# Router logits in plain fp32 from the residual, and 14 cells of the first expert's weights fetched earlier

## The chip, the cores and the metric

The kernel runs on one core of a Trainium2 chip. The metric is the device time of one execution, in microseconds; the median of several executions counts.

## What is computed

A trunk of two decoder layers over 256 tokens of width 1024, in fp32. Layer 0 is differential attention and a dense SwiGLU, layer 1 is an attention over blocks (here one block of 256, so plain causal attention with ALiBi) and a top-2-of-8 expert SwiGLU. The part that the change touches is the second layer's feed-forward:

```python
def moe_swiglu(h, router, w_gate, w_up, w_down):
    ...
    logits = (tok @ router).astype(jnp.float32)
    top_v, top_i = lax.top_k(logits, TOP_K_EXPERTS)
    w = jax.nn.softmax(top_v, axis=-1)
    gates = jnp.sum(jax.nn.one_hot(top_i, N_EXPERTS, dtype=jnp.float32) * w[..., None], axis=1)
    out = jnp.zeros_like(tok)
    for e in range(N_EXPERTS):
        out = out + gates[:, e:e + 1].astype(tok.dtype) * swiglu(tok, w_gate[e], w_up[e], w_down[e])
```

`tok` is the normalized residual. Each expert has w_gate and w_up of 1024x3584 and w_down of 3584x1024, 44 MB together, and all eight are read: 352 MB.

## The kernel before

**Weights and the ring.** All weights stream from HBM through a ring in SBUF of 7 slots of 8 cells; a cell is 128x512 fp32 (256 KB). SyncE issues the transfers in program order. Before each it waits until `group_used`, which TensorE counts up as it uses cells, says that the cells to be overwritten are done with. `NG` is the count at the end of the last product before the experts (attention's output projection of layer 1).

**Items.** The experts' work is cut into items. Item 0, 2, 4, 6 and 7 are "few" items (up to 64 tokens, plain fp32 products straight from the ring, `few_columns` and `few_down`), items 1, 3 and 5 are "big" ones (up to 128 tokens; ScalarE copies each cell to a rounded high half `whi`, VectorE subtracts it to a low half `wlo`, and TensorE makes three products, lines 1725 to 1727). The tokens of each expert decide which expert is worked on in which item; GpSimd builds the table. An item has 24 steps: gate's eight row blocks of seven cells, up's eight of seven cells, down's seven of eight cells: 168 cells in all (56 + 56 + 56). The big item's and the following few item's steps are interleaved in SyncE's and TensorE's order.

**Item 0.** Its expert is fixed (expert 0), so that its weights can be fetched before routing is known (`few_item(0, 0, ...)`, lines 701 to 728). Cells 0 to 55, all of gate, go to the ring. Cells 56 to 71, up's first two row blocks and two cells of the third, go to two further buffers, `ahead[0]` and `ahead[1]` of eight cells each, which share memory with tiles that are not in use at the time: `ahead[0]` with `whi`, `ahead[1]` with part of attention's tiles (q and k halves, values) and with `hhi`, `hlo`, `ihi` and `ilo`. Cells from 72 on go to the ring again, where gate's were. `few_used` gives the count for which SyncE waits, one for each row block; the block that holds cells of `ahead[1]` waits for `logit_mm` too.

**The router.** While the output projection of layer 1 ends, VectorE adds it to the transposed residual `resT` (`add_block`, lines 1598 to 1609). ScalarE rounds `resT` to high halves, put in `hhi` and `ihi` (`raw_hi`, line 981), VectorE subtracts for low halves, in `hlo` and `ilo` (`raw_lo`, line 1592). The router's weights `rt` are halved too, side by side in `rt_parts` (16 columns). TensorE (`logits`, line 1985) multiplies with `rt_parts` as the loaded operand, two products for each of eight row blocks, which gives 16 rows of 256 tokens. ScalarE copies them out (`logitT`, line 1002), and two small products with `sum_parts` (line 1997) turn them and add the halves: 128 tokens x 8 experts in `psA`, twice. VectorE finds the top two (lines 1615 to 1622) and sets `member`; TensorE counts the tokens of each expert (lines 2004 to 2008), VectorE makes `pick` from it (line 1626), and TensorE gathers item 0's rows with it (`gather_first`, line 2015). Between these, TensorE turns the residual back to rows (`turn_rows`, line 1974, 16 transposes), which ScalarE copies and squares (lines 1004 and 988) and VectorE copies (line 1631), and `keep_streaming` (line 1979) is a filler product. The first product of item 0 is at line 2100.

Of the kernel before, what the change touches and what calls it, by code (L numbers as in the profile page):

```python
# [30 lines left out]
P = 128  # L31
# [10 lines left out]
def trunk(nc, x, norm_mix, norm_ffn, diff_w_qkv, diff_w_o, diff_lambda, diff_subln, moba_w_qkv, moba_w_o,  # L42
# [143 lines left out]
    with ExitStack() as ctx:  # L186
        def sb(name, shape, dt=F32, stack=ctx):
            return stack.enter_context(nc.sbuf_tensor(name, shape, dt))

        def sem(name):  # L190
            return ctx.enter_context(nc.semaphore(name))
# [82 lines left out]
        sum_parts = sb("sum_parts", [2 * E, E])  # L274
        rs_of_slot = sb("rs_of_slot", [P, 1])
        ident_r = sb("ident_r", [P, P], F32R)
        rt_parts = sb("rt_parts", [P, KD, 2 * E], F32R)
        top = sb("top", [P, TB, E])
        top_at = sb("top_at", [P, TB, E], U32)
        logitT = sb("logitT", [2 * E, T])  # L280
# [103 lines left out]
        rt_split = sem("rt_split")  # L384
        block_done = sem("block_done")
        block_added = sem("block_added")
        thi_done = sem("thi_done")
        tlo_done = sem("tlo_done")
# [4 lines left out]
        logitT_out = sem("logitT_out")  # L393
# [56 lines left out]
        def blocks(t, first, n):  # L450
            return t[:, first:first + n, :].rearrange("p k t -> p (k t)")

        def T_part(which, first, n):
            return blocks(hid_parts(first // 4)[which], first % 4, n)

        def f(ap):
            return ap.bitcast(F32)
# [49 lines left out]
        def few_runs(i, j):  # L507
            runs = []
            for q in range(item_cells[j]):
                x = item_from[j] + q  # L510
                if isinstance(i, int) and i == 0 and CELLS <= x < CELLS + AHEAD_CELLS:
                    what, at = divmod(x - CELLS, GS)
                    what = 1 + what
                else:
                    what, at = 0, ring_cell(i, x)
                if runs and runs[-1][0] == what and runs[-1][1] + runs[-1][2] == at:
                    runs[-1][2] += 1
                else:
                    runs.append([what, at, 1, q])
            return [([ring_all, ahead[0], ahead[1]][what][:, at * W:(at + n) * W], q, n) for what, at, n, q in runs]  # L520

        def few_used(j):
            end = item_from[j] + item_cells[j]
            if end <= CELLS:
                return NG - CELLS + -(-end // GS) * GS
            return NG + max(end - CELLS - AHEAD_CELLS if end < 2 * CELLS + AHEAD_CELLS else end - CELLS, 0)
# [122 lines left out]
        def _(sp):  # L649
# [52 lines left out]

            def few_item(i, e, slots_of):
                for j in slots_of:
                    kind, at = item_slots[j]
                    first = isinstance(i, int) and i == 0
                    if first:
                        sp.wait_ge(group_used, few_used(j))
                        if item_from[j] <= CELLS + GS < item_from[j] + item_cells[j]:
                            sp.wait_ge(logit_mm, 1)  # L710
                    else:
                        sp.reg_add(used_past, used_past, item_cells[j])
                        sp.wait_ge(group_used, used_past)
                    if kind != "down":
                        w = moe_w_gate if kind == "gate" else moe_w_up
                        for to, q, n in few_runs(i, j):
                            sp.dma_start(to, w[0][e, at * P:(at + 1) * P, q * W:(q + n) * W]).then_inc(item_full[j], 16)
                        continue
                    dst = few_runs(i, j)[0][0]
                    if not isinstance(i, int) and j >= FS - 2:  # L720
                        for a, (b, half, g) in enumerate(DOWN_ROWS[at]):
                            sp.dma_start(dst[:, a * D:(a + 1) * D], few_down(e, b, half)[:, g * D:(g + 1) * D]).then_inc(
                                piece_full[j - FS + 2][a] if a < FBW - 1 else item_full[j], 16)
                        continue
                    for a, (b, half, g) in enumerate(DOWN_ROWS[at]):
                        if g == 0:
                            rows = BANKS[b] // P
                            sp.dma_start(dst[:, a * D:(a + rows) * D], few_down(e, b, half)).then_inc(item_full[j], 16)
# [21 lines left out]
        def _(act):  # L750
# [183 lines left out]
            act.wait_ge(rt_gained, 1)  # L934
            nc.scalar.copy(rt_parts[:, :, 0:E], rt[:, :, :]).then_inc(rt_split, 1)
# [44 lines left out]
            def raw_hi(first, n):  # L980
                nc.scalar.copy(T_part(0, first, n), blocks(resT, first, n)).then_inc(thi_done, n)

# [9 lines left out]
            for q in range(2):  # L992
                act.wait_ge(block_added, 2 * q + 2)
                raw_hi(2 * q, 2)
            act.wait_ge(block_added, 6)
            raw_hi(4, 2)
            for k in range(6, KD):
                act.wait_ge(block_added, k + 1)
                raw_hi(k, 1)
            row_square(0, 0)  # L1000
            act.wait_ge(logit_mm, 1)
            nc.scalar.copy(logitT[:, :], psA[0:2 * E, 0, 0:T]).then_inc(logitT_out, 1)
# [96 lines left out]
        def _(pool):  # L1099
# [73 lines left out]
            tt(sum_parts[:, :], ident[0:2 * E, 0:E], ident[0:2 * E, E:2 * E], ALU.add).then_inc(scales_set, 1)  # L1173
# [3 lines left out]
            pool.wait_ge(scales_set, 3)  # L1177
# [138 lines left out]
        def _(dve):  # L1316
# [273 lines left out]
            def raw_lo(first, n):  # L1590
                dve.wait_ge(thi_done, first + n)
                nc.vector.tensor_tensor(T_part(1, first, n), blocks(resT, first, n), f(T_part(0, first, n)),
                                        ALU.subtract).then_inc(tlo_done, n)

            halve_to(NG)
            dve.wait_ge(rt_split, 1)
            nc.vector.tensor_tensor(rt_parts[:, :, E:2 * E], rt[:, :, :], f(rt_parts[:, :, 0:E]),
                                    ALU.subtract).then_inc(rt_split, 1)
# [5 lines left out]
            for q in range(2):  # L1604
                raw_lo(2 * q, 2)
# [4 lines left out]
            raw_lo(4, 2)  # L1610
            for a in range(2):
                raw_lo(6 + a, 1)
            dve.wait_ge(logit_mm, 2)
# [106 lines left out]
        def _(pe):  # L1720
# [260 lines left out]
            def logits(first, last):  # L1981
                for k in range(first, last):
                    pe.wait_ge(tlo_done, k + 1)
                    for which in (0, 1):
                        ins = mm(psA[0:2 * E, 0, 0:T], rt_parts[:, k, :], T_part(which, k, 1),
                                 start=k == 0 and which == 0, stop=k == KD - 1 and which == 1)
                return ins

            pe.wait_ge(rt_split, 2)
# [4 lines left out]
            pe.wait_ge(scales_set, 3)  # L1994
            pe.wait_ge(logitT_out, 1)
            for tb in range(TB):
                ins = mm(psA[:, 1, tb * E:(tb + 1) * E], logitT[:, tb * P:(tb + 1) * P], sum_parts[:, :], start=True, stop=True)
            ins.then_inc(logit_mm, 1)
# [255 lines left out]
```

## Time and profile before

| | us |
|---|---|
| median of 3 executions | 1258.49 (1257.98 to 1259.1) |
| profiled execution | 1259.62 |
| its span, first to last instruction | 1257.8 |
| TensorE busy | 1234.0 (98%) |
| VectorE, ScalarE, GpSimd busy | 641.3, 562.0, 99.8 |
| read from HBM | 422.23 MB |
| TensorE's granted clock | 0.999 of full |

Times in a profile count from the first instruction of the span. The 1.8 us that the execution is longer than its span lie around it. A queue's name ends in q (SPq is SyncE's): such a row is the time in which transfers were issued, not the one in which they moved.

### The profile page before, as it was taken

The page shows a single profiled execution, that of the slowest core. Times are in us where ns is not written, and L with a number is a line of the kernel's source. Part 1 is how long each engine was busy: PE and PEld are TensorE (multiplying, and loading weights), DVE is VectorE, ACT ScalarE, POOL GpSimd, SP SyncE. Part 2 cuts the span into 40 slices and gives each one's busy share as a digit, 9 for nine tenths or more (in the row PEclk, how much of TensorE's full clock was granted, in tenths as well). Part 3 has the DMA queues.
Part 4 walks back from the last instruction along what each step waited for, and adds up shares of the span by engine and source line. Part 5 has one row for each costly group of instructions (what it writes and reads, how often), then busy time and mean ns, then how long its engine had stood idle before and what let it go on. Part 6 is the DMA issues. An engine that isn't in the chain of part 4 may idle for free.

```text
span 1257.8 us, 18674 instructions
## 1 busy us (share of the span) xinstructions
PE 1234.0 (98%) x7266; PEld 872.8 (69%) x7266; DVE 641.3 (51%) x788; ACT 562.0 (45%) x895; POOL 99.8 (8%) x260
## 2 busy tenths in 40 slices
PE   9998999999999999999999999999999999999887
PEld 8988999999999954487575457848447765733232
DVE  5787765555765400288383257838126855620011
ACT  6565454443655421388173158527027835500001
POOL 1000000000000074100001200000210000021000
PEclk9999999999999999999999999999999999999999
DMA  9933545357632299999999999999999999999997
GB/s 329 378 136 135 182 167 188 134 166 234 228 118 100 96 426 428 422 424 427 426 426 427 424 425 426 425 426 425 428 422 426 427 407 418 424 429 424 427 427 291
DMA packets 72136, 424.48 MB, mean 337 GB/s; under 512 B 5457, under 2 KB 24050, under 8 KB 48242
## 3 DMA queue, kind: packets, MB, share of 16 engines
q1 hardware_dynamic: 71696, 422.76, 83.0%
q8 instruction: 58, 0.95, 0.3%
q10 hardware_dynamic: 354, 0.54, 0.1%
q14 instruction: 28, 0.23, 0.0%
HBM read 422.23 MB, written 1.05 MB: 337 GB/s over the span
## 4 chain that ended last, share of the span: by engine, by line
PE 89%; DMA 5%; ACT 2%; DVE 2%; issue 1%; POOLq 0%; POOL 0%; ACTq 0%; DVEq 0%; SPq 0%
PE psB L2100 10%; PE psY L2115 9%; PE psA L2100 7%; PE psY L1725 7%; PE psY L1727 7%; PE psY L1726 7%; PE psB L1725 6%; PE psA L1725 5%; PE psB L1727 5%; PE psB L1726 5%; PE psA L1727 5%; PE psA L1726 5%; DMA ring<-in_moe_w_up 2%; DMA ring<-in_moe_w_down 2%; PE psY L2066 1%; PE psY L1873 1%
## 5 line engine op out<-in xcount | busy, mean ns | idle before, releaser
L1585 DVE TENSOR_TENSOR wlo<-ring,whi 128x2048 fp32r<-128x2048 f32 (+3 forms) x171 | 289.1, 1727 | 150.7 <-ACT whi L950 148.5
L950 ACT CAST whi<-ring 128x1024 fp32r<-128x1024 f32 (+1 forms) x276 | 259.5, 981 | 155.1 <-DMA ring<-in_moe_w_down 72.4
L1332 DVE TENSOR_TENSOR wlo<-ring,whi 128x1024 fp32r<-128x1024 f32 (+2 forms) x104 | 152.3, 1485 | 17.6 <-ACT whi L764 17.5
L764 ACT CAST whi<-ring 128x1024 fp32r<-128x1024 f32 (+1 forms) x134 | 133.4, 1023 | 60.0 <-PE psY L1727 28.3
L2100 PE MATMUL psB<-ring,resT 128*64 128x512 f32 x620 | 149.0, 598 | 7.4 <-DMA ring<-in_moe_w_up 5.4
L2100 PE MATMUL psA<-ring,resT 128*64 128x512 f32 (+1 forms) x624 | 113.9, 486 | 0.0
L1725 PE MATMUL psA<-xhi,whi 128*128 128x256 f32 x368 | 105.0, 285 | 2.6 <-DVE wlo L1332 1.2
L2100 PEld LDWEIGHTS psA<-ring,resT 128*64 128x64 f32 x624 | 44.8, 137 | 89.1 <-issue 89.1
L1725 PE MATMUL psB<-xhi,whi 128*128 128x256 f32 x368 | 106.4, 289 | 0.0
L1726 PE MATMUL psA<-xlo,whi 128*128 128x256 f32 x368 | 102.7, 279 | 0.0
L1726 PE MATMUL psB<-xlo,whi 128*128 128x256 f32 x368 | 102.7, 279 | 0.0
L1727 PE MATMUL psA<-xhi,wlo 128*128 128x256 f32 x368 | 102.6, 279 | 0.0
L1727 PE MATMUL psB<-xhi,wlo 128*128 128x256 f32 x368 | 102.6, 279 | 0.0
L2100 PEld LDWEIGHTS psB<-ring,resT 128*64 128x64 f32 x620 | 41.6, 136 | 75.7 <-issue 56.8
L1652 DVE TENSOR_TENSOR rowbuf<-psY,rowbuf 128x512 f32<-128x512 f32 x28 | 18.6, 688 | 141.1 <-PE psY L2066 141.1
L2115 PE MATMUL psY<-ring,hidT 128*64 128x512 f32 x320 | 72.1, 596 | 0.7 <-DMA ring<-in_moe_w_down 0.6
L1725 PEld LDWEIGHTS psA<-xhi,whi 128*128 128x128 f32 x368 | 69.2, 188 | 4.5 <-issue 3.3
L1725 PEld LDWEIGHTS psB<-xhi,whi 128*128 128x128 f32 x368 | 69.4, 189 | 0.0
L1726 PEld LDWEIGHTS psB<-xlo,whi 128*128 128x128 f32 x368 | 69.3, 188 | 0.0
L1726 PEld LDWEIGHTS psA<-xlo,whi 128*128 128x128 f32 x368 | 69.2, 188 | 0.1
L1727 PEld LDWEIGHTS psB<-xhi,wlo 128*128 128x128 f32 x368 | 69.2, 188 | 0.0
L1727 PEld LDWEIGHTS psA<-xhi,wlo 128*128 128x128 f32 x368 | 69.2, 188 | 0.0
(382 smaller groups left out, 2147.1 us busy)
## 6 DMA issues: line engine op xcount, KB each, us to landing
ring<-in_moe_w_down SPq DMA_DIRECT2D x50, 2048.0 KB, 15.6
ring<-in_moe_w_up SPq DMA_DIRECT2D x53, 1792.0 KB, 18.1
ring<-in_moe_w_gate SPq DMA_DIRECT2D x50, 1792.0 KB, 14.9
ring<-in_moe_w_gate SPq DMA_DIRECT2D x13, 1024.0 KB, 15.5
ring<-in_ffn_w_gate SPq DMA_DIRECT2D x5, 2048.0 KB, 8.8
ring<-in_ffn_w_up SPq DMA_DIRECT2D x5, 2048.0 KB, 7.8
ring<-in_ffn_w_down SPq DMA_DIRECT2D x5, 2048.0 KB, 8.0
ring<-in_moe_w_gate SPq DMA_DIRECT2D x13, 768.0 KB, 14.0
```

The lines of the kernel that those rows point to most:

```text
L764: nc.scalar.copy(hi_of(m, size), part_of(ring, s, g, size)).then_inc(hi_done, size)
L950: nc.scalar.copy(hi_of(NG + m, size), item_part(ring, m, size)).then_inc(hi_done, size)
L1332: nc.vector.tensor_tensor(part_of(wlo, s, g, size), part_of(ring, s, g, size), f(hi_of(m, size)), ALU.subtract).then_inc(lo_done, size)
L1585: nc.vector.tensor_tensor(item_part(wlo, m, size), item_part(ring, m, size), f(hi_of(NG + m, size)), ALU.subtract).then_inc(lo_done, size)
L1652: nc.vector.tensor_tensor(r, slot_bank(half), r, ALU.add).then_inc(add_done, 1)
L1725: mm(ps, xh, wh, start=start, stop=False, skip_group_check=shared)
L1726: mm(ps, xh, wl, start=False, stop=False, skip_group_check=shared)
L1727: return mm(ps, xl, wh, start=False, stop=stop, skip_group_check=shared)
L1873: ins = mm(psY[:, 3, i * wide:(i + 1) * wide], probsT[:, u % 2, i * (tb + 1) + kb, :], val[:, kb, c:c + wide], start=kb == 0, stop=kb == tb)
L2066: mm(slot_bank(half), s_, y, start=True, stop=True).then_inc(scatter_mm, 1)
L2100: ins = mm(few_bank(b)[half * FEW:(half + 1) * FEW, to:to + end - x], few_in[:, k, :], raw[:, x - q * W:end - q * W], start=k == 0, stop=k ...
L2115: ins = mm(psY[half * FEW:(half + 1) * FEW, 0, :], few_act[b][:, g * P + left * FEW:g * P + (left + 1) * FEW], raw[:, a * D + half * W:a * ...
```

## The change

The logits are computed from `resT` and `rt` in plain fp32, with `resT` as the loaded operand: for each of the eight row blocks two products of eight columns, one for each half of the tokens. They come out with tokens in rows, so that nothing is turned or added afterwards. The halves, `rt_parts`, `sum_parts`, `logitT` and their steps are gone from ScalarE, VectorE, GpSimd and TensorE.

`ahead[1]` no longer holds halves of the residual, and the two further buffers change places: cells 56 to 63 go to `ahead[1]`, 64 to 71 to `ahead[0]`. Cells 42 to 47 (gate's seventh row block without its last cell) wait for `group_used` as gate's sixth does. Behind them, once the last product of attention's weights and values is counted (`pv_done`), SyncE fetches up's first row block and one cell of the second, to `ahead[1]`. The last cell of gate's seventh row block follows when `NG` is reached. The count is now worked out for each transfer instead of each row block, and nothing waits for `logit_mm`.

```diff
-                if runs and runs[-1][0] == what and runs[-1][1] + runs[-1][2] == at:
+                last_dense = isinstance(i, int) and i == 0 and x == CELLS - GS
+                if runs and runs[-1][0] == what and runs[-1][1] + runs[-1][2] == at and not last_dense:
...
-            return [([ring_all, ahead[0], ahead[1]][what][:, at * W:(at + n) * W], q, n) for what, at, n, q in runs]
-
-        def few_used(j):
-            end = item_from[j] + item_cells[j]
+            return [([ring_all, ahead[1], ahead[0]][what][:, at * W:(at + n) * W], q, n) for what, at, n, q in runs]
+
+        def first_used(j, q, n):
+            end = item_from[j] + q + n
             if end <= CELLS:
                 return NG - CELLS + -(-end // GS) * GS
             return NG + max(end - CELLS - AHEAD_CELLS if end < 2 * CELLS + AHEAD_CELLS else end - CELLS, 0)
...
+            def early_ahead(j, q):
+                return CELLS <= item_from[j] + q < CELLS + GS
+
+            def first_rows(j, a):
+                to, q, n = few_runs(0, j)[a]
+                k = item_slots[j][1]
+                sp.dma_start(to, moe_w_up[0][0, k * P:(k + 1) * P, q * W:(q + n) * W]).then_inc(item_full[j], 16)
...
-                    if first:
-                        sp.wait_ge(group_used, few_used(j))
-                        if item_from[j] <= CELLS + GS < item_from[j] + item_cells[j]:
-                            sp.wait_ge(logit_mm, 1)
-                    else:
+                    if first and kind == "down":
+                        sp.wait_ge(group_used, first_used(j, 0, GS))
+                    elif not first:
...
                         for to, q, n in few_runs(i, j):
+                            if first and early_ahead(j, q):
+                                continue
+                            if first and item_from[j] + q == CELLS - GS:
+                                sp.wait_ge(pv_done, 2 * UNITS)
+                                first_rows(item_slot["up", 0], 0)
+                                first_rows(item_slot["up", 1], 0)
+                            if first:
+                                sp.wait_ge(group_used, first_used(j, q, n))
...
-            act.wait_ge(rt_gained, 1)
-            nc.scalar.copy(rt_parts[:, :, 0:E], rt[:, :, :]).then_inc(rt_split, 1)
...
-            def raw_hi(first, n):
-                nc.scalar.copy(T_part(0, first, n), blocks(resT, first, n)).then_inc(thi_done, n)
...
-            for q in range(2):
-                act.wait_ge(block_added, 2 * q + 2)
-                raw_hi(2 * q, 2)
-            act.wait_ge(block_added, 6)
-            raw_hi(4, 2)
-            for k in range(6, KD):
-                act.wait_ge(block_added, k + 1)
-                raw_hi(k, 1)
             row_square(0, 0)
-            act.wait_ge(logit_mm, 1)
-            nc.scalar.copy(logitT[:, :], psA[0:2 * E, 0, 0:T]).then_inc(logitT_out, 1)
...
-            def raw_lo(first, n):
-                dve.wait_ge(thi_done, first + n)
-                nc.vector.tensor_tensor(T_part(1, first, n), blocks(resT, first, n), f(T_part(0, first, n)),
-                                        ALU.subtract).then_inc(tlo_done, n)
...
             def logits(first, last):
                 for k in range(first, last):
-                    pe.wait_ge(tlo_done, k + 1)
-                    for which in (0, 1):
-                        ins = mm(psA[0:2 * E, 0, 0:T], rt_parts[:, k, :], T_part(which, k, 1),
-                                 start=k == 0 and which == 0, stop=k == KD - 1 and which == 1)
+                    pe.wait_ge(block_added, max(k + 1, 4))
+                    for tb in range(TB):
+                        ins = mm(psA[:, 1, tb * E:(tb + 1) * E], resT[:, k, tb * P:(tb + 1) * P], rt[:, k, :],
+                                 start=k == tb == 0, stop=k == KD - 1, skip_group_check=True)
                 return ins
 
-            pe.wait_ge(rt_split, 2)
+            pe.wait_ge(rt_gained, 1)
             logits(0, 4)
             turn_rows(0, 0)
             logits(4, KD).then_inc(logit_mm, 1)
             turn_rows(0, 1)
-            pe.wait_ge(scales_set, 3)
-            pe.wait_ge(logitT_out, 1)
-            for tb in range(TB):
-                ins = mm(psA[:, 1, tb * E:(tb + 1) * E], logitT[:, tb * P:(tb + 1) * P], sum_parts[:, :], start=True, stop=True)
-            ins.then_inc(logit_mm, 1)
```

Two places show how the order moves. First SyncE's queue from gate's sixth row block to up's third, before (the last three of "x6" are gate's sixth, seventh and eighth row block):

```order
L717 DMA ring<-in_moe_w_gate 128x3584 [waits group_used]
L717 DMA ring<-in_moe_w_gate 128x512 [waits group_used]
L717 DMA ring<-in_moe_w_gate 128x3072
L717 DMA ring<-in_moe_w_gate 128x3584 [waits group_used] x6
L717 DMA ahead<-in_moe_w_up 128x3584 [waits group_used]
L717 DMA ahead<-in_moe_w_up 128x512 [waits logit_mm,group_used]
L717 DMA ahead<-in_moe_w_up 128x3072
L717 DMA ahead<-in_moe_w_up 128x1024 [waits group_used]
L717 DMA ring<-in_moe_w_up 128x2560
```

The same in the changed kernel (line numbers are its own; the last of "x4" is gate's sixth row block):

```order
L722 DMA ring<-in_moe_w_gate 128x3584 [waits group_used] x4
L722 DMA ring<-in_moe_w_gate 128x3072 [waits group_used]
L700 DMA ahead<-in_moe_w_up 128x3584 [waits pv_done]
L700 DMA ahead<-in_moe_w_up 128x512
L722 DMA ring<-in_moe_w_gate 128x512 [waits group_used]
L722 DMA ring<-in_moe_w_gate 128x3584 [waits group_used]
L722 DMA ahead<-in_moe_w_up 128x3072 [waits group_used]
L722 DMA ahead<-in_moe_w_up 128x1024 [waits group_used]
L722 DMA ring<-in_moe_w_up 128x2560 [waits group_used]
```

Gate's seventh row block is cut in 3072 and 512 columns; between the pieces stand up's first row block and the first cell of its second, which stood behind gate's eighth.

Then TensorE's queue around the second half of the logits, before (L1985 the split products, L1974 the transposes, L1997 the sum of the halves, L2004 the first count):

```order
L1974 MATMUL psY<-ident,resT 128x128 x4
L1985 MATMUL psA<-ihi,rt_parts 16x256
L1985 MATMUL psA<-ilo,rt_parts 16x256
...
L1974 MATMUL psY<-ident,resT 128x128 x4
L1997 MATMUL psA<-sum_parts,logitT 128x8 x2
L1974 MATMUL psY<-ident,resT 128x128 x4
L1974 MATMUL psB<-ident,resT 128x128 x4
L1979 MATMUL psY<-resT,ident 128x128
L2004 MATMUL psA<-member,pickT 128x8
```

And the whole of it in the changed kernel (L1961 the logits, L1950 the transposes, L1955 keep_streaming, L1975 the first count):

```order
L1961 MATMUL psA<-rt,resT 128x8 x8
L1950 MATMUL psY<-ident,resT 128x128 x4
L1961 MATMUL psA<-rt,resT 128x8 x8
L1950 MATMUL psY<-ident,resT 128x128 x8
L1950 MATMUL psB<-ident,resT 128x128 x4
L1955 MATMUL psY<-resT,ident 128x128
L1975 MATMUL psA<-member,pickT 128x8
```

Sixteen products of 256 columns and two of eight are replaced by sixteen of eight columns, at the same places; the transposes stay, and eight of them now follow each other.

## Rows read from the trace of the kernel before

**Rows 1.** The page: TensorE's busy time; the dense layer's transfers, KB each, us to landing
```profile
PE 1234.0 (98%) x7266; PEld 872.8 (69%) x7266; DVE 641.3 (51%) x788; ACT 562.0 (45%) x895; POOL 99.8 (8%) x260
...
ring<-in_ffn_w_gate SPq DMA_DIRECT2D x5, 2048.0 KB, 8.8
```
**Rows 2.** Windows: length, busy of PE, PEld, DVE, ACT, POOL, clock, DMA share, GB/s
```profile
429.00:437.00 8.00, 7.91 (x68) 7.69 (x67) 3.90 (x7) 2.44 (x7) 1.94 (x23) 1.00 0.01 3
...
447.00:1160.00 713.00, 712.13 (x3366) 425.25 (x3368) 350.10 (x278) 315.88 (x425) 79.48 (x172) 1.00 1.01 424
...
1160.00:1236.50 76.50, 68.25 (x334) 24.50 (x331) 4.98 (x8) 6.24 (x17) 0.73 (x1) 1.00 1.00 425
```
**Rows 3.** TensorE's waits (total us, times, longest), 447 to 1160, then after 1160
```profile
PE psB L1725 <- DVE wlo L1585: 0.9, 3, 0.3
...
PE psB L2100 <- DMA ring<-in_moe_w_up: 5.4, 5, 1.1
```
**Rows 4.** Timeline of SyncE: start, length, queue, line, transfer, how many
```profile
422.35 15.53 SPq L717 DMA_DIRECT2D ring<-in_moe_w_gate  x3
...
437.07 0.80 SPq L717 DMA_DIRECT2D ring<-in_moe_w_gate  x2
...
450.78 14.99 SPq L717 DMA_DIRECT2D ring<-in_moe_w_up  x7
```
**Rows 5.** Issue to landing: at 385; L717 up to 432; at 450.8
```profile
ring<-in_moe_w_gate SPq DMA_DIRECT2D x1, 1792.0 KB, 6.8
...
DMA to landing us min/median/max: 2.7/7.2/7.5
...
ring<-in_moe_w_up SPq DMA_DIRECT2D x1, 1280.0 KB, 11.9
```
**Rows 6.** Issue to landing of the transfers issued at 609, 1028 and 1034
```profile
ring<-in_moe_w_gate SPq DMA_DIRECT2D x1, 1792.0 KB, 12.7
...
ring<-in_moe_w_gate SPq DMA_DIRECT2D x1, 1792.0 KB, 9.6
...
ring<-in_moe_w_down SPq DMA_DIRECT2D x1, 2048.0 KB, 9.7
```
**Rows 7.** Windows: the stretch behind the issue at 1034
```profile
1035.00:1040.00 5.00, 5.00 (x28) 1.90 (x26) 0.00 (x0) 0.00 (x0) 0.00 (x0) 1.00 0.94 313
```
**Rows 8.** DMA queues, 1034 to 1035: packets, MB, share of 16 engines
```profile
q8 instruction: 1, 0.02, 6.4%
```
**Rows 9.** Timeline of TensorE: attention's last product with values
```profile
423.43 1.10 PE L1873 MATMUL psY<-val,probsT 128*128 128x64 f32 x8 [0.24 <-ACT probsT L815]
```
**Rows 10.** Timeline of TensorE: first split product, first count, first product of item 0
```profile
436.87 0.28 PE L1985 MATMUL psA<-hhi,rt_parts 128*16 128x256 f32 x1
...
441.99 0.24 PE L2004 MATMUL psA<-member,pickT 128*128 128x8 f32 x1
...
447.14 0.65 PE L2100 MATMUL psB<-ring,resT 128*64 128x512 f32 x2
```
**Rows 11.** The chain of waits, in order of time: start, us, what
```profile
441.29 0.44 PE psB L1974 x4
...
443.22 1.82 PE psA L2015 x16
```
**Rows 12.** Groups of instructions, 443 to 446.9: busy us, mean ns of one
```profile
L2015 PE MATMUL psA<-pick,rowbuf 128*128 128x64 f32 x16 | 2.0, 276 | 0.0
```
**Rows 13.** Timelines of ScalarE and VectorE behind the logits
```profile
440.06 1.01 ACT L1004 COPY rowbuf<-psY 128x1024 f32<-128x1024 f32 x1
...
440.74 0.25 DVE L1615 MAX8 top<-psA 128x8 f32<-128x8 f32 x2 [1.64 <-PE psA L1997]
...
441.67 0.17 DVE L1622 TENSOR_TENSOR member<-chosen 128x16 fp32r<-128x16 f32 x1
...
443.69 0.68 DVE L1631 COPY rowbuf<-psB 128x512 f32<-128x512 f32 x1
```
**Rows 14.** Timeline of GpSimd: the first step behind the tables, its idle time ahead
```profile
492.55 0.19 POOL L1288 COPY slot_now<-few_slot_at 128x1 f32<-128x1 f32 x1 [11.28 <-ACT row_and_weight L1041]
```

More of the change, by code:

```diff
@@ L273, in trunk @@
         pickT = sb("pickT", [P, T], F32R)
-        sum_parts = sb("sum_parts", [2 * E, E])
         rs_of_slot = sb("rs_of_slot", [P, 1])
         ident_r = sb("ident_r", [P, P], F32R)
-        rt_parts = sb("rt_parts", [P, KD, 2 * E], F32R)
         top = sb("top", [P, TB, E])
         top_at = sb("top_at", [P, TB, E], U32)
-        logitT = sb("logitT", [2 * E, T])
         count = pickT[:, :].rearrange("p (a t) -> p a t", a=2)
@@ L383, in trunk @@
         rt_gained = sem("rt_gained")
-        rt_split = sem("rt_split")
         block_done = sem("block_done")
         block_added = sem("block_added")
-        thi_done = sem("thi_done")
-        tlo_done = sem("tlo_done")
         rowT_mm = sem("rowT_mm")
@@ L392, in trunk @@
         logit_mm = sem("logit_mm")
-        logitT_out = sem("logitT_out")
         count_set = sem("count_set")
@@ L451, in blocks @@
             return t[:, first:first + n, :].rearrange("p k t -> p (k t)")
-        def T_part(which, first, n):
-            return blocks(hid_parts(first // 4)[which], first % 4, n)
         def f(ap):
@@ L1172, in _ @@
             tt = nc.gpsimd.tensor_tensor
-            tt(sum_parts[:, :], ident[0:2 * E, 0:E], ident[0:2 * E, E:2 * E], ALU.add).then_inc(scales_set, 1)
             pool.wait_ge(sq_done, 4 * 3 + TB)
@@ L1176, in _ @@
             pool.wait_ge(pos_set, 1)
-            pool.wait_ge(scales_set, 3)
+            pool.wait_ge(scales_set, 2)
             link(tt(key[:, :], pos[:, TB, :], tie[:, :], ALU.add))
@@ L1588, in item_halve @@
                 return done
-            def raw_lo(first, n):
-                dve.wait_ge(thi_done, first + n)
-                nc.vector.tensor_tensor(T_part(1, first, n), blocks(resT, first, n), f(T_part(0, first, n)),
-                                        ALU.subtract).then_inc(tlo_done, n)
             halve_to(NG)
-            dve.wait_ge(rt_split, 1)
-            nc.vector.tensor_tensor(rt_parts[:, :, E:2 * E], rt[:, :, :], f(rt_parts[:, :, 0:E]),
-                                    ALU.subtract).then_inc(rt_split, 1)
             dve.wait_ge(block_done, 1)
@@ L1603, in _ @@
             add_block(psB[:, 0, :], 2, block_added, 2)
-            for q in range(2):
-                raw_lo(2 * q, 2)
             dve.wait_ge(group_used, NG)
@@ L1609, in _ @@
                 nc.vector.tensor_tensor(r, psB[:, 1, a * T:(a + 1) * T], r, ALU.add).then_inc(block_added, 1)
[L1610 to L1613, printed above, removed]
+            dve.wait_ge(logit_mm, 1)
             for tb in range(TB):
```

## Prediction

> **What bounds the kernel now.** I began with the page. TensorE works 98% of the span [rows 1]; the windows then show the DMA engines full as well from 447 us on, at about 425 GB/s [rows 2]. Two resources look like the bound at once, and which of them it is must be settled before a transfer that comes earlier can be given a price. From 429 to 437 us the DMA engines stand still (3 GB/s) [rows 2]: that is the hole which the change fills. From 447 to 1160 TensorE works 712.13 of 713 us [rows 2], and its waits there name VectorE's splits, 0.9 us, and no transfer [rows 3]. From 1160 to 1236.5 it works only 68.25 of 76.5 us [rows 2], and there it waits for weights, 5.4 us in one row alone [rows 3]. So TensorE sets the pace up to 1160, and the stream of weights sets the end.
>
> What ties the two is the ring. SyncE may issue a transfer only when TensorE has used up the cells that it overwrites. How far the stream's backlog covers this is read from issue to landing. A transfer of seven cells (1792 KB) that meets idle DMA engines lands after 6.8 to 7.5 us, 7.2 in the middle (the 2.7 is a single cell) [rows 5]: 4.3 us of data (1.835 MB at 424 GB/s) and 2.9 fixed. While the engines are full it takes longer, and the excess is the queue ahead of it. This excess shrinks: 12.7 us at 609, 9.6 at 1028, and the eight cells (2048 KB) at 1034 take 9.7 [rows 6]. Eight cells on idle engines should take 7.2 + 0.6 = 7.8 (bounds 6.8 + 0.6 = 7.4, and 8.8, the dense layer's transfers of that size [rows 1]). So some 1.9 us of queue is left at 1034 (bounds 0.9 and 2.3). The window there agrees: DMA share 0.94, 313 GB/s [rows 7]; some engines already run dry. On this place the forecast hangs.
>
> **The early transfers.** The 14 cells are 14 x 0.262 = 3.67 MB, 8.7 us of DMA. Six (gate's seventh slot without its last cell) wait for the same count as gate's sixth slot and go out right behind it, at 422.7 [rows 4]. The other eight wait for attention's last product, which ends at 423.43 + 1.10 = 424.5 [rows 9]. Behind the sixth slot's landing (422.35 + 7.2 = 429.5 [rows 4, 5]) they fill the engines to 438.2, and the hole is closed. The stream would be 8.7 us ahead. But little may follow: at 437.07 [rows 4] SyncE can issue 1 + 7 + 6 + 2 = 16 cells, 9.9 us of data, which run from 439 to 449. The 17th lies in gate's first slot, used up 3 us after item 0 starts; its issue is at 450.78 now [rows 4]. Here the engines run dry for some 2 us. Its transfer of five cells then lands at 451.3 + 2.9 + 3.1 = 457.3, against 450.78 + 11.9 = 462.7 [rows 4, 5]: the lead is 5.4 us, already 3.3 less. SyncE's new wait for pv_done holds behind it only transfers that wait for 437.07 anyway, and its wait for the logits, removed, held two that stood behind a full queue: neither moves anything.
>
> **The logits on TensorE.** Its path runs from the first split product at 436.87 to the first count (L2004) at 441.99, 5.12 us [rows 10]. In it stood 16 split products, the two that sum the halves, 16 transposes, two records of keep_streaming, and the waits for VectorE's splits, ScalarE's copy and member. In it will stand: the 16 transposes, 0.11 each by the row of four in 0.44, 1.76 us [rows 11]; keep_streaming's two, 0.22; and 16 fp32 products of eight columns with 128x128 weights. The trace has none of that shape; the nearest is the gather (L2015), fp32 too, with 128x128 weights and 64 columns: its eight products stand as 16 records in 1.82 us [rows 11], 0.114 each. So 16 products are 32 records, 3.64 us. Together 5.62: the count starts 0.5 us later. Nothing else holds it: VectorE's table work from top to member takes 440.74 to 441.84, 1.1 us [rows 13], and the 12 transposes and two records that now stand behind the logits take 1.5. Item 0 starts at 447.14 + 0.5 = 447.6 [rows 10].
>
> Bounds: 32 records can hardly cost less than a transpose's 0.11 [rows 11], 3.5 us, start +0.4; above, a record's own length, 276 ns [rows 12], if nothing overlapped: 8.8 us, start +5.7. I take 0.114, since that row has the same load and kind of product.
> The Trainium skill, "FP8 and Floating Point Precision", TensorE Precision Notes, gives true fp32 four passes through the array. The gather's row, two records a product, speaks against four at full price; by that rule, 64 records, the start would move by 4.1 us.
>
> **What lies beside it.** ScalarE loses six casts and logitT's copy, VectorE six subtractions, GpSimd an addition of 0.2 us in idle time: they bring nothing but the waits counted above, since TensorE's queue is the longer one. Late instead is rowbuf's copy (L1004, at 440.06 [rows 13]): its transposes now end at 441.5, so this copy and the squares behind it come 1.5 us later. VectorE's second copy (L1631), which waits for the last square, then ends not at 443.69 + 0.68 = 444.4 [rows 13] but near 445.2 (it waited for VectorE itself before); the gather's second half needs it at 443.22 + 1.82 + 0.5 = 445.5 [rows 11]. Cover 0.3 us; if it is gone, the excess adds to the 0.5. GpSimd's tables begin 1.5 us later; it then idles 11.28 us behind them [rows 14]: nothing.
>
> **The sum.** TensorE is 0.5 us late from item 0 to 1160, and so is every permission. The stream's lead melts wherever the queue does not cover it. At 1034 it is the queue that stood there: eight cells issued at 1034.18 + 0.5 on idle engines land at 1042.5, against 1034.18 + 9.7 = 1043.9 [rows 4, 6]. That is 1.4 us early; afterwards the same transfers follow at the same rate, the queue covers the rest, and the end moves with them. One packet of program code (6.4% of 16 engines' us, 1.0 us of one engine [rows 8]) falls just there and may hold the slowest engine now as before, which leaves 0.4. I take the middle, 0.9. The profiled execution took 1259.62 us (span 1257.8), 1.1 above the median of 1258.49; so 1258.7 for a profiled one and **1257.6** for the median. The 8.7 us are fetched early and nearly all given back, because the ring is full sooner.
> The Trainium skill, "DMA: Bandwidth & Descriptors", Anatomy of one DMA, fits 2.0 us + bytes/436 GB/s, an estimate of 6.8 us for eight cells; by it 2.9 us of queue stood at 1034 and the gain would be 2.4. The rows have 6.8 to 7.5 us for seven cells already [rows 5], so I stay with them.
>
> **The rivals.** (1) *The lead is kept*: the queue at 1034 is longer than issue-to-landing shows, as the slowest engine decides that. For it: the DMA engines are full almost everywhere, and TensorE's 8.25 us of idle time after 1160 leave room. Against: 313 GB/s at 1035. The 5.4 us of the first pause would reach the end: 1253.1. (2) *Slower*: the fp32 products cost more than the gather's. All of it falls on the only path into item 0, and the ring passes it on. Unoverlapped it is +5.7, less the 1.4 us of queue (the middle of 1.9 and 0.9): +4.3, 1262.8; with four records a product (+4.1): +2.7, 1261.2. It decides from 0.22 us a record. For it: 16 products add into one bank in turn. Against: so do the gather's. (3) *The early transfers don't come early*, held to 437 by pv_done or the count. Then only the +0.5 is left: 1259.0. Rows 9 speak against.
>
> **How the numbers follow.** The tie at 1034: 0.73. Lead kept: 0.11. Slower: 0.07, half for each price. No early transfer: 0.06. The rest, 0.03, lies on both sides. A measurement tells apart about 0.2%, 2.5 us: faster is under 1256.0, slower over 1261.0. Faster: rival 1 and the tie's lower tail, 0.17. Slower: rival 2 and an upper tail, 0.09. Same: 0.74. Range: below, the bound of 2.3 us of queue, and 0.6 if the eighth cell costs nothing while engines are dry, less 0.5, is 2.4 early; the runs lie 1.1 apart: 1255.0. Above, all the lead lost is +0.5, with the same 1.1: 1260.1. That leaves out rivals 1 and 2, 0.18.
>
> **What would show it.** Right: full DMA from 424 to 438; a dip near 449 to 453; item 0 starting at 447.5 to 447.9; 32 records at 0.11 us in the logits; issue to landing near 7 to 8 us at 1028 and 1034, with a DMA share of 0.95 or less also near 610 and 820; TensorE still without waits for weights to 1160. Wrong: TensorE's idle time after 1160 down to 4 us or less (rival 1); records over 0.2 us (rival 2); a hole before 437 still there (rival 3).

## The result, and the profile after

The change is slower, by some 0.4%: 1265.85 us, the median of 17 runs (1257.26 to 1268.32), against 1258.64 us for the kernel before in the same rounds (17 runs, 1257.91 to 1259.45). The ratio is 1.004 (95% interval 1.0029 to 1.0051); here and below it weighs all executions and is not the ratio of the two medians, which is 1.0057. The forecast, 1257.6 with a range up to 1260.1, was wrong.

The spread says more than the median. The kernel before stays within 1.5 us; the change spreads over 11. Sorted, with the granted TensorE clock averaged over each execution:

| executions | time, us | mean granted clock |
|---|---|---|
| 3 | 1257.26, 1257.45, 1257.75 | 0.998 to 0.999 |
| 4 | 1260.06, 1260.27, 1260.61, 1261.95 | 0.997 to 0.998 |
| 10 | 1265.81 to 1268.32 | 0.990 to 0.993 |

The profiled execution is one of the ten: 1267.18 us, span 1265.4, against 1259.62 and 1257.8 before. From its page come TensorE's busy time, and, of the 40 slices, the clock, the DMA share and GB/s:

```profile
PE 1243.4 (98%) x7280; PEld 881.9 (70%) x7280; DVE 638.6 (50%) x782; ACT 559.1 (44%) x888; POOL 99.3 (8%) x259
...
PEclk9999999999999979999999999999999999999999
DMA  9933545347523659999999999999999999999997
GB/s 330 374 137 132 197 171 173 128 167 256 210 109 118 241 243 421 422 426 426 408 428 425 425 425 425 425 397 425 429 423 426 426 412 415 425 427 425 426 426 297
```

TensorE is 9.4 us busier than in [rows 1] and still 98% busy. One slice of 40 has a 7 in the clock's row, the one from 443 to 475 us. The windows of the change split it up (length; busy time of PE, PEld, DVE, ACT and POOL; granted clock; DMA share; GB/s):

```profile
424.00:429.00 5.00, 4.83 (x40) 4.71 (x40) 2.13 (x4) 1.18 (x4) 1.03 (x7) 1.00 0.96 407
429.00:437.00 8.00, 7.92 (x69) 7.89 (x68) 2.56 (x5) 0.00 (x0) 1.42 (x19) 1.00 0.94 395
437.00:440.00 3.00, 3.00 (x25) 3.00 (x24) 0.18 (x1) 0.69 (x2) 0.00 (x0) 0.82 0.87 285
440.00:445.00 5.00, 5.00 (x26) 5.00 (x25) 1.06 (x9) 2.71 (x7) 0.24 (x1) 0.50 1.00 429
445.00:450.00 5.00, 5.00 (x23) 4.82 (x23) 1.75 (x4) 0.73 (x5) 3.67 (x12) 0.50 0.58 243
450.00:456.00 6.00, 6.00 (x25) 4.46 (x26) 0.16 (x1) 1.51 (x7) 4.65 (x20) 0.50 0.01 3
456.00:460.00 4.00, 4.00 (x14) 1.28 (x12) 0.00 (x0) 0.00 (x0) 3.69 (x18) 0.57 0.00 0
460.00:465.00 5.00, 5.00 (x28) 1.82 (x26) 0.00 (x0) 0.00 (x0) 3.71 (x17) 1.00 0.79 290
...
460.00:1170.00 710.00, 709.14 (x3354) 424.38 (x3352) 349.91 (x277) 315.29 (x421) 70.36 (x134) 1.00 1.00 421
...
1170.00:1245.00 75.00, 68.32 (x334) 24.72 (x332) 4.98 (x8) 6.23 (x17) 0.73 (x1) 1.00 1.01 425
```

The granted clock is 1.00 (2.4 GHz) up to 437, 0.82 over 437 to 440, 0.50 (1.2 GHz) from there to 456, and 1.00 again from 460. A mean of 0.82 over 3 us of two levels puts the fall at about 438.9, one of 0.57 over 4 us puts the rise at 459.4: 20.5 us at half speed. TensorE is busy in all of it, 3.00 of 3.00 and 5.00 of 5.00 us; nothing waits. What the work was is in the chain of waits (start, us, what):

```profile
436.38 1.69 PE psA L1961 x16
438.07 0.49 PE psY L1950 x4
438.56 2.75 PE psA L1961 x16
441.31 1.80 PE psY L1950 x8
443.11 0.85 PE psB L1950 x4
...
446.31 3.31 PE psA L1986 x16
449.62 3.41 PE psY L1986 x16
...
453.78 3.61 PE psB L2071 x8
457.39 2.36 PE psA L2071 x8
```

L1961 is the new logits product. Its first 16 records take 1.69 us, 0.106 each; the second 16, in which the clock falls, 2.75. Four transposes then take 0.85 us instead of 0.44, and the gather's first half 3.31 instead of 1.82 [rows 11]. Item 0 still begins at half speed. TensorE's timeline has the logits' first product and item 0's first product:

```profile
436.22 1.85 PE L1961 MATMUL psA<-rt,resT 128*128 128x8 f32 x16
...
453.71 3.68 PE L2071 MATMUL psB<-ring,resT 128*64 128x512 f32 x8
```

The second line is 6.6 us later than the 447.14 of before [rows 10]. The first shows that two profiled executions are not aligned to the last tenth: the logits start at 436.22 here and at 436.87 before [rows 10], and nothing ahead of them that TensorE does was changed. Counted from the logits' first product, item 0 is 7.2 us late (17.49 against 10.27 us). Item 0's first 16 records take 3.61 + 2.36 = 5.97 us; in the chain of the kernel before the same took 1.87 + 1.29 = 3.16. SyncE's timeline shows the stream of weights that waits for them:

```profile
424.00 0.81 SPq L700 DMA_DIRECT2D ahead<-in_moe_w_up  x2
...
436.42 0.81 SPq L722 DMA_DIRECT2D ring<-in_moe_w_gate  x2
...
459.80 15.36 SPq L722 DMA_DIRECT2D ring<-in_moe_w_up  x7
...
1043.51 0.33 SPq L676 DMA_DIRECT2D ring<-in_moe_w_down  x1
```

The eight cells of up go out at 424.0, and the hole of [rows 2] is filled (DMA share 0.96 and 0.94). Then the ring is full. From about 449 to 459.8 the DMA engines have nothing (share 0.01, 0.00), until item 0 frees cells: 9.0 us later than at 450.78 in [rows 4]. The same is left at the last step that the prediction looked at, where the kernel before has this line:

```profile
1034.18 0.33 SPq L685 DMA_DIRECT2D ring<-in_moe_w_down  x1
```

The change is 9.3 us late there, and 7.6 us at the end of the span (10.0 and 8.3 counted from the logits' first product). The whole loss thus arises between 438.9 and 459.4; afterwards 1.7 us come back. Issue to landing of the transfers issued at 618, 1037 and 1043 in the change:

```profile
ring<-in_moe_w_gate SPq DMA_DIRECT2D x1, 1792.0 KB, 8.2
...
ring<-in_moe_w_gate SPq DMA_DIRECT2D x1, 1792.0 KB, 8.8
...
ring<-in_moe_w_down SPq DMA_DIRECT2D x1, 2048.0 KB, 7.7
```

In [rows 6] they took 12.7, 9.6 and 9.7: the excess has shrunk, and the last takes what the prediction gave for eight cells on idle engines, 7.8.

### The profile page after: what moved, and what is told of

It reads as the page before. It is cut to its first block, busy times and chain, and to the rows that moved or that the text cites. A ratio compares the mean times of both kernels' runs of the same rounds, so it can differ in the third digit from the quotient of the medians.

```text
span 1265.4 us, 18681 instructions
## 1 busy us (share of the span) xinstructions
PE 1243.4 (98%) x7280; PEld 881.9 (70%) x7280; DVE 638.6 (50%) x782; ACT 559.1 (44%) x888; POOL 99.3 (8%) x259
## 4 chain that ended last, share of the span: by engine, by line
PE 90%; DMA 4%; ACT 2%; DVE 2%; issue 1%; POOLq 0%; POOL 0%; ACTq 0%; DVEq 0%; SPq 0%
PE psB L2071 10%; PE psY L2086 9%; PE psA L2071 7%; PE psY L1701 7%; PE psY L1703 7%; PE psY L1702 7%; PE psB L1701 5%; PE psA L1701 5%; PE psB L1703 5%; PE psB L1702 5%; PE psA L1703 5%; PE psA L1702 5%; DMA ring<-in_moe_w_down 2%; DMA ring<-in_moe_w_up 2%; PE psY L2037 1%; PE psY L1849 1%
```

## The experiments

The question was why the clock falls in some executions. Theory C: the new logits leave TensorE with records that are busy but stream few columns, 32 of them with 16 transposes between and behind. Theory T, the rival: the other half of the change, transfers that now run from 424 to 438, disturbs TensorE or its clock. All comparisons are against the kernel before, on the same chip. Some kernels compute products whose result is thrown away; none leaves part of the computation out.

**The new logits alone.** The change, with the transfers and waits of the kernel before.

```diff
...
-                if runs and runs[-1][0] == what and runs[-1][1] + runs[-1][2] == at and not last_dense:
+                if runs and runs[-1][0] == what and runs[-1][1] + runs[-1][2] == at:
...
-                    if first and kind == "down":
-                        sp.wait_ge(group_used, first_used(j, 0, GS))
-                    elif not first:
+                    if first:
+                        sp.wait_ge(group_used, few_used(j))
+                        if item_from[j] <= CELLS + GS < item_from[j] + item_cells[j]:
+                            sp.wait_ge(logit_mm, 1)
+                    else:
```

> The logits of the change with the transfers of before (up's first slots fetched after 437 us, logit_mm waited for). Theory C: the eight-column fp32 products alone make the chip halve TensorE's clock (1.2 instead of 2.4 GHz) behind them: in most executions a mean granted clock of 0.990 to 0.993 and 1264 to 1269 us, as the whole change has. Theory T: the early transfers beside the projection's dense products do it: clock 0.998 to 0.999 and 1259.1 us (0.5 us later into item 0, nothing else).

1260.73 us (1258.22 to 1268.4, 12 runs), ratio 1.0034 (1.0017 to 1.0052): seven between 1258.22 and 1260.88 with clocks of 0.997 to 0.999, five between 1266.19 and 1268.4 with 0.990 to 0.992. The long falls are there, but in five of twelve executions, where the expectation had most, and the median lies below its 1264 to 1269. The profiled execution is one of the seven, and has a short fall (windows):

```profile
430.00:436.00 6.00, 6.00 (x54) 6.00 (x53) 1.98 (x3) 0.00 (x0) 0.91 (x15) 1.00 0.02 4
436.00:440.00 4.00, 4.00 (x39) 4.00 (x38) 0.75 (x2) 0.69 (x2) 0.00 (x0) 1.00 0.52 158
440.00:444.00 4.00, 4.00 (x24) 4.00 (x23) 1.00 (x8) 2.06 (x5) 0.24 (x1) 0.57 1.02 437
444.00:450.00 6.00, 6.00 (x48) 5.13 (x49) 1.97 (x5) 2.79 (x14) 4.21 (x14) 1.00 0.98 421
```

0.57 over 4 us is 3.4 us at half speed, and 1.7 us lost. That is in line with its item 0, which starts at 448.88 against 447.14 [rows 10]. The fall is there though the DMA engines stood still from 430 to 436 (share 0.02), so the early transfers are not needed for it and the logits are enough. Whether those transfers make a long fall more likely (10 of 17 executions with them, 5 of 12 without) so few executions don't decide.

**The early transfers alone.** The change with the logits of before; the split halves go to `xhi`, `xlo` and `whi`'s last cells, which no early transfer overwrites.

```diff
+        def T_part(which, first, n):
+            if first < 4:
+                return blocks((xhi, xlo)[which], first, n)
+            at = slice((first - 4) * T, (first - 4 + n) * T)
+            return blocks(whi, 8 + 2 * which, 2)[:, at]
```

> The transfers of the change with the logits of before; the halves of the residual lie in xhi, xlo and the last four cells of whi instead of ahead[1]. Theory C: clock 0.998 to 0.999 in all executions and, since item 0 starts as before, 0.9 to 1.9 us less than before by the queue at 1034: 1256.7 to 1257.7 us. Theory T: clock of 0.990 to 0.993 and over 1264 us.

1258.37 us (1256.95 to 1258.74, 11 runs), ratio 0.9995 (0.9986 to 1.0004), all clocks 0.998 or 0.999. So this half alone does no harm. Its median is 0.3 us lower (1258.68 to 1258.37), which the interval does not tell from nothing; 0.9 to 1.9 had been forecast. Its window shows the hole filled, and then the dry stretch that the prediction put there:

```profile
430.00:436.00 6.00, 6.00 (x54) 6.00 (x53) 2.32 (x4) 1.48 (x3) 1.19 (x19) 1.00 1.02 431
...
450.00:455.00 5.00, 5.00 (x30) 1.93 (x28) 0.00 (x0) 0.00 (x0) 4.20 (x22) 1.00 0.72 248
```

The transfers issued at 1028 and 1034 still take this long to land:

```profile
ring<-in_moe_w_gate SPq DMA_DIRECT2D x1, 1792.0 KB, 10.4
...
ring<-in_moe_w_down SPq DMA_DIRECT2D x1, 2048.0 KB, 9.8
```

**More columns, the same loads (64 and 128).** If few columns are the cause, products with more must keep the clock. `wide64` multiplies each block of `resT` with all 64 columns of `rt` instead of its own eight, and shifts the result by eight for each block, so that the wanted eight meet in the same place (VectorE reads them from there); `wide128` does so with `rt` twice, 128 columns.

```diff
...
-                        ins = mm(psA[:, 1, tb * E:(tb + 1) * E], resT[:, k, tb * P:(tb + 1) * P], rt[:, k, :],
+                        at = tb * P + (KD - k) * E
+                        ins = mm(psA[:, 1, at:at + KD * E], resT[:, k, tb * P:(tb + 1) * P], blocks(rt, 0, KD),
```

> The whole change, but each of the 16 fp32 products takes all 64 columns of rt instead of 8 (each block shifted by 8 columns in PSUM so that the wanted 8 add up at one place; the others are thrown away). As many records, the same loads, the same length (1.8 us for 16 records at the full clock). Theory C in the form that the columns streamed decide: the clock falls in fewer executions, median under 1262 us, perhaps 1257.5. Rival C2, that the length of the stretch of weight loads decides whatever is streamed: as the change, median about 1266 us.

> As wide64 with 128 columns (rt taken twice). Columns decide: clock 0.998 to 0.999 in all executions and 1257.5 to 1258.2 us (32 records at 0.114 to 0.124 us). C2, the loads decide: about 1266 us as before.

1258.2 us (1257.36 to 1260.04, 11 runs), ratio 0.9999 (0.999 to 1.0008), and 1258.27 us (1257.05 to 1259.24, 11 runs), 0.9996 (0.9987 to 1.0005). In all 22 executions the mean clock is 0.998 or 0.999, and none is over 1260.04 us. A long fall is thus in none; a short one can hide behind a mean of 0.998 (the change's 1260.06 has it too), and the one execution of `wide64` at 1260.04 may be such a case. From the chain of `wide128`, then its window:

```profile
436.89 1.78 PE psA L1962 x16
...
439.11 1.79 PE psA L1962 x16
```

```profile
440.00:444.00 4.00, 4.00 (x37) 3.78 (x35) 2.02 (x11) 2.63 (x7) 0.24 (x1) 1.00 1.04 442
```

Loads, records, order and transfers are those of the change; only the columns differ. A record costs 0.111 us with 128 columns and 0.106 with eight, and the clock stays at 1.00 where it was 0.50. In these kernels, then, the columns, up to 128, hardly touch a record's price (that the load sets it is the likely reason, which no run varied alone), and the columns streamed, not the loads, decide whether the clock is kept. Item 0 starts at 447.35, where 447.6 was forecast.

**The same products twice.** Each narrow product is issued once more, into columns that nobody reads.

```diff
...
+                        mm(psA[:, 1, 4 * P - (tb + 1) * E:4 * P - tb * E], resT[:, k, tb * P:(tb + 1) * P], rt[:, k, :],
+                           start=k == tb == 0, stop=k == KD - 1, skip_group_check=True)
...
```

> The change with every eight-column product issued twice (the second result goes to unused columns of PSUM and is thrown away): the stretch of narrow products is twice as long. Theory C: the clock falls in every execution or nearly so, the median is 1268 to 1275 us (the stretch itself adds 3.6 us at the full clock and 7.3 at the half). If the fall were a matter of chance unrelated to the narrow products, half of the executions would stay at 0.998 or more, at 1257.5 + 3.6 = 1261 us.

1268.03 us (1266.19 to 1272.59, 6 runs), ratio 1.0085 (1.0068 to 1.0102). Now every execution loses clock (0.996 to 0.990). With twice the narrow records it is all of six, with one set 14 of 17; six executions do not tell these apart (if 14 in 17 were the rule, all six would fall in a third of such trials), so the run agrees with theory C and adds little to it. Nor is the low stretch longer: four of the six have a mean of 0.994 to 0.996, above the 0.990 to 0.993 of the change's ten. Its windows also show the way back:

```profile
440.00:442.00 2.00, 2.00 (x11) 2.00 (x11) 0.00 (x0) 0.17 (x1) 0.00 (x0) 0.50 1.02 437
...
450.00:455.00 5.00, 5.00 (x36) 4.95 (x35) 1.81 (x4) 2.83 (x11) 2.21 (x7) 0.78 0.02 3
```

0.78 over 5 us puts the rise at about 452, before item 0's first product at 456.74.

**Without the fillers, before and wide.** The `keep_streaming` products (128 and 256 columns, results unused) now looked like what keeps the clock up. `before_nofill` is the kernel before without both, `wide128_nofill` the same with `wide128`.

```diff
-            keep_streaming(P)
...
-            keep_streaming(T)
```

> The kernel before without its two filler products (keep_streaming of 128 and of 256 columns). Theory C: the transposes, counts and gather around them are sparse too, so some executions lose the clock (mean 0.99, over 1264 us), the others take 0.5 to 0.8 us less than before, since item 0 starts earlier by the fillers' 0.22 + 0.54 us. Rival: the fillers are not needed, all executions take 1257.9 to 1258.1 us at 0.998 or more.

> wide128 without the two fillers. If the wide products carry the clock through the stretch, clock 0.998 to 0.999 and 0.7 us less than wide128's 1258.3, so 1257.5 us. If the fillers carry it behind the logits, executions at 0.99 and 1264 us or more come back.

`before_nofill`: 1262.55 us (1258.53 to 1263.98, 12 runs), ratio 1.0029 (1.002 to 1.0037). Three executions lie at 1258.5 to 1258.8 with a clock of 0.998, nine at 1261.7 to 1264.0 with 0.993 to 0.996. The kernel before stands close to losing its clock, and the two fillers keep it. `wide128_nofill`: 1258.29 us (1257.18 to 1260.77, 11 runs), ratio 1.0001 (0.9992 to 1.0009), with two executions at 1260.2 and 1260.8 (0.998, 0.997). The 1257.5 that I expected without the fillers' own time is missed: their removal brings nothing.

**The same products, spread out.** The first eight narrow products are placed between the last wide products of the projection; `interleave_wide` does so with 128 columns.

```diff
+                    if fb >= 2:
+                        for _ in range(2 if n == end - 1 else 1):
+                            pe.wait_ge(block_added, 4)
+                            logit(*early.pop(0))
...
-            logits(0, 4)
```

> The change with its first eight narrow products set one by one between the last dense products of the output projection, so that no more than eight narrow products stand together; TensorE's total work is the same. Theory C (a stretch of narrow work, not the products as such, costs the clock): falls in fewer executions than the change's 10 of 17 and logits_only's 5 of 12, median under 1260 us. If the products as such did it: as the change.

> interleave with the 128 columns of wide128, fillers kept. Theory C: no execution under a clock of 0.998; 1257.8 to 1258.3 us, by R no faster than wide128 since TensorE's work is the same.

`interleave`: 1258.48 us (1257.36 to 1261.63, 11 runs), ratio 1.0004 (0.9995 to 1.0013): eight executions keep the clock (1257.4 to 1258.7), three lose a little (1261.0 to 1261.6; 0.997 to 0.998), none 8 us. Only 3 of 11 lose clock, against 14 of 17, though all 16 products are still narrow: what counts is how many stand together, not each by itself. `interleave_wide`: 1258.47 us (1257.15 to 1259.76, 11 runs), 0.9999 (0.999 to 1.0008); with the clock kept there is nothing more to win here.

**Is there queue for lateness, or lead?** The prediction let a queue at 1034 absorb some lateness of TensorE. Four fillers of 512 columns ahead of the second `keep_streaming` make item 0 late and leave the clock alone, once in the kernel before, once in `wide128`, whose stream has the lead.

```diff
+            for _ in range(4):
+                keep_streaming(W)
             keep_streaming(T)
```

> The kernel before with four more filler products of 512 columns ahead of its keep_streaming of 256, 4.3 us of dense work (two records of 0.54 us each) that makes TensorE late into item 0 and touches nothing else. Theory R (TensorE sets the pace up to 1160 us and the ring passes its lateness to the end, less the queue of 0.9 to 2.3 us that stands at 1034): 1258.6 + 4.3 less 0.9 to 2.3 = 1260.6 to 1262.0 us, clock 0.998 or more. Rival: the stream of weights alone sets the end, its lead hides the 4.3 us: 1258.6 to 1259 us.

> wide128 with the same four filler products. Theory R: the early transfers leave no more queue than the ring allows, so nothing covers the lateness: 1258.3 + 4.3 = 1262.6 us, at most 0.5 less. Rival: the 8.7 us of weights that are fetched early cover it: 1258.3 to 1259 us.

`before_late`: 1261.18 us (1260.19 to 1262.78, 11 runs), ratio 1.0021 (1.0012 to 1.003). Its first split product and item 0's first product:

```profile
436.00 0.28 PE L1985 MATMUL psA<-hhi,rt_parts 128*16 128x256 f32 x1
...
449.63 1.94 PE L2100 MATMUL psB<-ring,resT 128*64 128x512 f32 x8
```

Item 0 stands 2.5 us behind the 447.14 of [rows 10], but this execution was 0.9 us ahead when the split products began. From there to item 0 it takes 13.63 us against 10.27: the fillers cost 3.4 us, 0.42 for each of their eight records, not the 4.3 that I had priced. (With 512 columns, then, the columns do set a record's price.) Of these 3.4 the profile passes 2.0 to the end of the span (822.9 us from the first split product, against 820.9 before), and the median 2.5 (interval 1.5 to 3.8). So some 0.9 to 1.4 us are absorbed, about what the prediction gave the queue at its lower end, though the interval also allows none. That the time fell into the forecast 1260.6 to 1262.0 is partly luck, since the fillers' price was too high.

`wide128_late`: 1261.96 us (1261.16 to 1263.53, 11 runs), 1.0027 (1.0017 to 1.0036). Its logits start at 435.95 and item 0 at 449.92, 13.97 us against the 10.62 of `wide128`: again 3.4 us more. The profile passes 2.3 of them to the end of the span, the medians, from two different rounds, 3.7. The rival, that the weights fetched early cover the lateness, is out; whether a third of it or nothing is covered stays open.

No version beats the kernel before: `early_only` and `wide128` are nearest to it, at 0.9995 and 0.9996, with 1 inside both intervals.

## Why the prediction was wrong

**The step that failed** is "The logits on TensorE", at "Item 0 starts at 447.14 + 0.5 = 447.6". Item 0 started at 453.71 in the profile. The records were counted and priced well: 32 of them, forecast 0.114 us each, measured 0.106 at full clock and 0.111 in `wide128`; and where the clock is kept, item 0 starts at 447.35. But every price was a row at 2.4 GHz, and the step never asked whether the clock would stay there. It fell in the second run of these products, and everything up to the first products of item 0 took twice its time: 6.1 us more up to 453.71 than forecast, 2.8 us more in its first 16 records. With the 0.5 that was forecast this is 9.4 us against the kernel before, of which 7.6 us reached the end of the span.

The Trainium skill, "TensorE: Matmul & The Clock Gate", HAM oscillation — how this bites in real kernels, puts the falls of the kernel that it treats down to TensorE's waits for transfers between short bursts of products. No such wait stands here: TensorE is busy for 5.00 of 5.00 us in the windows at a clock of 0.50. Whoever looks for idle gaps alone, as I did, passes over this case.

**What was at hand and not used.** I booked the two fillers at 0.22 us and did not ask what they are for. A product whose result nobody reads has a purpose, and `before_nofill` shows it: some 4 us of its median. And the list of what is removed held a second entry beside time: 16 products that stream 256 columns each [rows 10] went, 16 that stream eight came. That exchange was read as a matter of microseconds only.

**The rivals.** The second had the right side and the right place, "the only path into item 0", but a wrong mechanism, dearer records (it was to decide from 0.22 us a record), at 0.07 in all. The profile has 0.106, and the 1267.18 of the profiled execution lies beyond its 1262.8. The first rival, the lead kept, fell: no kernel with the clock kept came near 1253.1. The third fell with the issue at 424.0.

**The early transfers: right up to item 0.** Out at 424.0, the engines full until 437, 16 cells more, then a dry stretch. With `wide128` and `early_only`, which keep the clock, DMA shares of 0.67 and 0.72 from 450 to 455 show the pause.

**The sum: its gain is not shown.** "I take the middle, 0.9" rested on 0.9 to 2.3 us of queue at 1034. Four kernels have the early transfers and the fillers and keep the clock in every execution or nearly so: `early_only`, `wide64`, `wide128` and `interleave_wide`. Their medians lie only 0.2 to 0.5 us below the kernel before, and every interval (1.8 us gained to 0.5 lost for `early_only`) holds both nothing and the 0.9. So the lead is given back nearly whole, as forecast, and the 0.9 is neither shown nor refuted. The sign that was to carry it, the eight cells issued near 1034 landing after 7 to 8 us, comes in some profiles and not in others. In `wide64` and in `interleave`:

```profile
ring<-in_moe_w_down SPq DMA_DIRECT2D x1, 2048.0 KB, 8.0
...
ring<-in_moe_w_down SPq DMA_DIRECT2D x1, 2048.0 KB, 7.9
```

In `early_only` they take 9.8 us and in `wide128` 10.3, in `before_nofill`, without any lead, 9.0. The excess over 7.8 is therefore not simply a queue that a lead takes away. For lateness some of it does work as one: about 1 of 3.4 us is absorbed in `before_late`, and the change, 9.3 us late, gets 1.7 back with the landing down to 7.7; but in `twice`, just as late at that step (1043.73), they still land after 9.4 us. What the excess is made of, I have not settled.

The estimate of 6.8 us beside the sum was misapplied: the fit in the Trainium skill, "DMA: Bandwidth & Descriptors", Anatomy of one DMA, is for transfers that GpSimd issues, and these are SyncE's. The shortest landing of eight cells near that step in the profiles is the change's 7.7 us.

**As a whole**: where the clock is kept, the prediction's mechanism gives about what was measured: `wide128` takes 1258.27 us, 0.7 above the 1257.6 and inside the range. (The change's own three best executions, 1257.3 to 1257.8, are the fast end of a wide spread and prove less.) The missing case came in 14 of 17 executions, ten of them with the long stretch, and no rival of the prediction names it.

## What to carry to other kernels

Before wide products are exchanged for narrow ones, look at the granted clock over the stretch and at what else stands beside it: a TensorE that is 100% busy can still lose half its clock, and all that follows pays. Where a record costs the same with few columns as with more, as here up to 128, wider products cost next to nothing (64 or 128 columns instead of eight here), and spreading the narrow ones among dense work helps nearly as much. Products that look useless may be what holds the clock; take one out only with ten or so executions timed, since a median of three can miss a state that appears in some of them.

## What was unexpected in the hardware

- The clock fell from 2.4 to 1.2 GHz in the midst of unbroken work (busy 3.00 of 3.00 us from 437 to 440), and was back only at 459.4, some 5.7 us into item 0's products of 512 columns.
- It is a matter of the execution: the same program kept the clock in 3 of 17, lost it shortly in 4 and for long in 10. The low stretch was 20.5 us in the change's profile and 3.4 us in `logits_only`'s, and in `logits_only` and `twice` it ended before item 0 began. What tells these apart stays open.
- An fp32 product with a load of 128x128 costs nearly the same with eight columns and with 128: 1.69 and 1.78 us for 16 records at the full clock.
